# Expert fetches of 4 slots x 32 tokens in place of 1 slot x 128 tokens, with the weighting matmul in quarters

## The chip, the cores and the metric

One NeuronCore of one Trainium2 chip runs the whole program. The metric is device microseconds (us) of that core. The kernel before takes 4421.82 us, the median of three runs (4420.11 to 4427.95). All arithmetic is float32.

## The reference, cut to what matters

The program is one layer of a network over 9 tiles of 128 tokens (1 context tile, 8 latent tiles), D = 1024. Input projection, mLSTM and attention come first; the change touches only the last stage, `peer`, a retrieval of single-neuron experts:

```
q = (x @ w_q).reshape(N, 8, 256)                       # 8 heads
sa, sb = scores of the two halves of q against 128 keys each
va, ia = top_k(sa, 16);  vb, ib = top_k(sb, 16)        # "sides": 16 per token
cand = va[..., :, None] + vb[..., None, :]             # 256 candidates per head
top, pos = top_k(cand, 16);  eidx = ia*128 + ib at pos # 8 heads x 16 = 128 slots per token
gates = softmax(top)
a   = gelu(einsum('pd,phkd->phk', x, u_tab[eidx]))     # one dot product per token and slot
out = einsum('phk,phkd->pd', gates * a, v_tab[eidx])   # weighted sum of 128 rows per token
y   = x1 + gate2 * out
```

Each token thus reads 128 rows of u and 128 rows of v, 1024 floats each. They lie side by side in one table `uv` of 2048 floats a row, 8 KB.

## The kernel before, in words

The stage `peer` runs 9 tiles one after the other. A tile has 128 slots, done as 8 turns of 16 (`PAIR`). Slot i of a tile means: for each of the 128 tokens (one per partition) its i-th expert. One slot goes through these engines:

- GpSimd (POOL) copies 8 columns of indices (L1294) and issues one indirect DMA per slot (L1301). It gathers 128 rows of 8 KB, 1 MB, into one of 8 ring buffers (`ring`, `GROUP` = 8). Before it may issue, it waits for `s_pv`, which TensorE raises when the slot that used the buffer 8 slots earlier has been accumulated.
- VectorE (DVE) waits for the landing, multiplies the u half by the token's row in `h2` and sums it (L1528, one custom instruction and a read of the accumulator) to `dot`.
- Slots go on in batches of 2: ScalarE (ACT) applies gelu (L1407), VectorE multiplies by the gates (L1533), ScalarE makes one 128x128 diagonal matrix per slot, identity times the weight of each token (L1412).
- TensorE (PE) multiplies that diagonal by the v half of the ring buffer in two halves of 512 columns and adds into two PSUM accumulators `acc` (L1345). A float32 matmul is issued as two pairs of weight load and matmul, so that a slot is 4 matmul instructions. The second half raises `s_pv`.

Beside this, the engines prepare the retrieval of the next tile. TensorE does one query block of 8 matmuls (L1325) after each batch of 2 slots in the first 16 of the 64 batches of a tile, and 4 score blocks (L1336). VectorE takes one piece of top-k work (`next(work)`: L1452 to L1513) per batch, between the dot products of the batch and its product with the gates, from the fifth batch of turn 1 on. For tile 0 the retrieval runs ahead of the first fetch.

At a tile's end TensorE closes the accumulation (L1367), VectorE multiplies by `gate2` and adds the residual (L1554, L1556), SyncE (SP) stores y and loads the next x1 (L1266, L1268). The next tile's `h2` is loaded (L1264) into the one `h2` buffer when the last dot product of the tile is done; VectorE's next tile starts with a wait for it. Tiles 1 to 7 are one hardware loop; tiles 0 and 8 stand outside it.

The order of the work is written out by hand: each engine has its own instruction stream, and semaphores tie them. DMAs of SP and of POOL share the core's 16 DMA engines.

Of the kernel before, what the change touches and what calls it, by code (L numbers as in the profile page):

```python
# [14 lines left out]
P = 128  # L15
D = 1024
# [15 lines left out]
NEG = -1e30  # L32
C1 = P + 1


# [1134 lines left out]
def peer(nc, g, io):  # L1170
# [10 lines left out]
    with ExitStack() as ctx:  # L1181
# [15 lines left out]
        idf = sb("pe_idf", [P, NSIDE, TOPK])  # L1197
        cand = sb("pe_cand", [P, PH, TOPK * TOPK])
        crest = rest[:].rearrange("p (h s) k -> p h (s k)", s=2)
# [30 lines left out]
        s_sc = sem("pe_scores_ready")  # L1230
        s_top = sem("pe_sides_done")
        s_mid = sem("pe_dve_chain")
# [17 lines left out]
        with nc.Block() as block:  # L1250
            @block.sync
            def _(sp):
                flat = h2T[:].rearrange("p k n -> p (k n)")
                sp.dma_start(subT[:], io.subT).then_inc(s_small, 16)
                sp.dma_start(flat, g.h2T_dram[0]).then_inc(s_hT, 16)
                for k in range(KD):
                    sp.dma_start(w_q[:, k, :], io.w_q[k * P:(k + 1) * P, :]).then_inc(s_wq, 16)
                sp.dma_start(h2[:], g.h2_dram[0]).then_inc(s_h, 16)
# [12 lines left out]
                sp.dma_start(flat, g.h2T_dram[1]).then_inc(s_hT, 16)  # L1271
                with sp.Fori(0, TILES - 2) as t:
                    sp.wait_ge(s_q, t * NG + 2 * NG)
                    sp.dma_start(flat, g.h2T_dram[t + 2]).then_inc(s_hT, 16)
                    after(t)
                after(TILES - 2)
                sp.wait_ge(s_out, TILES)
                sp.dma_start(io.y[TILES - 1], x1[:]).then_inc(s_st, 16)
                sp.wait_ge(s_st, TILES * 16)

            @block.gpsimd
            def _(pool):
# [4 lines left out]
                def turn(t, r, first=False):  # L1287
                    n = t * TURNS + r
                    for half in range(2):
                        if not first:  # L1290

                            pool.wait_ge(s_dot, n * PAIR - PAIR + GROUP * (half + 1))
                            pool.sem_inc(g.s_tick, 1)
                        pool.tensor_copy(idg[half][:], g.eidx[:, t, bass.ds(r * PAIR + half * GROUP, GROUP)]).then_inc(s_idx, 1)  # L1294
                        pool.wait_ge(s_idx, n * 2 + (half + 1))
                        for j in range(GROUP):
                            i = half * GROUP + j
                            if not (first and half == 0):
# [17 lines left out]
            def _(pe):  # L1316
# [22 lines left out]
                def turn(t, r, retrieve=False):  # L1339
                    n = t * TURNS + r  # L1340
                    for i in range(PAIR):
                        pe.wait_ge(s_diag, n * PAIR + (i + 1))

                        for b in range(2):
                            mm = pe.matmul(acc[b][:], diag[:, i % GROUP, :], ring[i % GROUP][:, D + b * 512:D + (b + 1) * 512],  # L1345
                                           start=False, stop=False)
                        mm.then_inc(s_pv, 1)
                        m = r * NB + i // BATCH if retrieve else 0
                        if retrieve and i % BATCH == 1:

                            if m < NSIDE:
                                query(t + 1, m // 4, m % 4)
                            if m >= 7 and (m - 7) % 4 == 0 and (m - 7) // 4 < NG:
                                scores(t + 1, (m - 7) // 4)

# [13 lines left out]

                pe.wait_ge(s_const, 2)  # L1370
                pe.wait_ge(s_small, 16)
# [13 lines left out]
            def _(act):  # L1385
# [6 lines left out]
                def out(t, b, first=False):  # L1392
                    act.wait_ge(s_c, t * NG + (b + 1))
                    if not first:
                        act.wait_ge(s_top, t * NG + (b + 1 - NG))
                    act.activation(sc[:, 4 * b:4 * b + 4, :], cP[b % 2][:], ACT.Copy).then_inc(s_sc, 1)
# [5 lines left out]
                def turn(t, r, first=False, retrieve=False):  # L1402
                    n = t * TURNS + r
                    for q in range(NB):
# [4 lines left out]
                        for i in range(q * BATCH, (q + 1) * BATCH):  # L1409
                            if not (first and i < GROUP):  # L1410
                                act.wait_ge(s_pv, n * PAIR + (i - GROUP + 1))
                            act.activation(diag[:, i % GROUP, :], g.ident[:], ACT.Copy, scale=w[:, i:i + 1]).then_inc(s_diag, 1)  # L1412
                        m = r * NB + q if retrieve else 0
# [23 lines left out]
                out(0, NG - 1, True)  # L1437
                gate_exp(0)
                tile(0, True)
                with act.Fori(1, TILES - 1) as t:  # L1440
# [4 lines left out]
            def _(dve):  # L1445


                def top16(c, rows, src, left, v, ix, last_sem=None):

# [15 lines left out]
                    for r in rows[2:]:  # L1465
                        ins = dve.max_index(ix[:, r, 0:8], v[:, r, 0:8], src[:, r, :])
                        if last_sem is not None and r == end:
                            ins.then_inc(last_sem, 1)
                    for r in rows[:-1]:
# [4 lines left out]
                def retrieval(c, t):  # L1474
                    for b in range(NG):
                        dve.wait_ge(s_sc, t * NG + (b + 1))
                        dve.sem_inc(g.s_tick, 1)
                        yield from top16(c, range(4 * b, 4 * b + 4), sc, rest, val, idx, s_top)

                    v4 = val[:].rearrange("p (h s) k -> p h s k", s=2)  # L1480
                    c4 = cand[:].rearrange("p h (a b) -> p h a b", a=TOPK)
                    c.link(dve.tensor_tensor(c4, v4[:, :, 0, :].unsqueeze(3).to_broadcast([P, PH, TOPK, TOPK]),
# [14 lines left out]
                    i4 = idf[:].rearrange("p (h s) k -> p h s k", s=2)  # L1497
                    for side, hit in enumerate((cand[:], crest)):
                        h3 = hit.rearrange("p h (a b) -> p (h a) b", a=TOPK)
# [13 lines left out]
                    dve.tensor_tensor(g.gates[:, t, :].rearrange("p (h k) -> p h k", h=PH), gex[:],  # L1513
                                      gsum[:].unsqueeze(2).to_broadcast([P, PH, TOPK]), ALU.mult).then_inc(s_route, 1)
                    dve.wait_ge(s_route, t + 1)
# [20 lines left out]
                def tile(t, cnd, more=True):  # L1536
                    dve.wait_ge(s_h, t * 16 + 16)
                    dve.sem_inc(g.s_tick, 1)
# [16 lines left out]
                    dve.wait_ge(s_gated, t * 2 + 2)  # L1555
                    dve.tensor_tensor(x1[:], x1[:], gated[:], ALU.add).then_inc(s_out, 1)  # L1556

                dve.wait_ge(s_const, 2)
                c = Count(dve, s_mid, LINKS, 0, g.s_tick)
# [172 lines left out]
```

## Time and profile before

| | |
|---|---|
| median of three runs | 4421.82 us |
| span of the profiled execution, first to last instruction | 4419.0 us |
| the profiled execution's own time | not listed apart from its span |
| stage `peer`, from the first fetch to the end | 1389.7 to 4419 us |
| indirect fetches | 1152, 1208.03 MB |
| PE busy, whole span | 3525.3 us (80%) |
| DVE / ACT / POOL busy | 2394.0 / 887.8 / 1616.3 us |

The profile page is one execution. Its 40 slices give, for each engine, the busy share in tenths. "PEclk" is TensorE's granted clock as a share of 2.4 GHz, "DMA" the mean busy share of the 16 DMA engines, and "GB/s" what they moved. "Idle before" is the time an engine stood still ahead of an instruction, with what released it. A busy share of the whole span mixes stages; the tables by window show one stage at a time.

### The profile page before, as it was taken

How to read it: one execution, taken by the hardware profiler on the slowest of the kernel's cores; microseconds unless marked ns; L12 is line 12 of the kernel's file. 1: busy time of each engine (PE TensorE's matmuls, PEld its weight loads, DVE VectorE, ACT ScalarE, POOL GpSimd, SP SyncE). 2: the span in 40 equal slices, each digit the busy share in tenths (PEclk: the TensorE clock that was granted, in tenths of full speed). 3: DMA queues.
4: the chain of work that ended last, by engine and by line, in shares of the span. 5: the costliest groups of instructions: out<-in, count | busy, mean ns of one | idle time of the engine just before them, and what ended most of it. 6: DMA issues, size and time to landing. Idle time of an engine off the chain costs nothing.

```text
span 4419.0 us, 43120 instructions
## 1 busy us (share of the span) xinstructions
PE 3525.3 (80%) x11157; PEld 1783.5 (40%) x11157; DVE 2394.0 (54%) x5673; ACT 887.8 (20%) x2523; POOL 1616.3 (37%) x1434
## 2 busy tenths in 40 slices
PE   8899778888864878877977977977977977977777
PEld 1444366555543423423523523522522522522222
DVE  1232354333316675674684685685584585585554
ACT  1111123322311221121121221121121121222111
POOL 0000011111102454454454454454445455445554
PEclk9899877777777999999999999999999999999999
DMA  9101123111134999999999999999999999999998
GB/s 368 56 34 45 55 92 119 38 47 38 47 125 172 410 418 417 404 419 387 403 416 390 400 417 391 398 420 397 391 418 417 371 418 420 372 420 417 415 421 360
DMA packets 219388, 1343.70 MB, mean 304 GB/s; under 512 B 22938, under 2 KB 33818, under 8 KB 69786
## 3 DMA queue, kind: packets, MB, share of 16 engines
q0 software_dynamic: 165888, 1208.03, 66.9%
q1 hardware_dynamic: 45628, 108.76, 6.8%
q10 hardware_dynamic: 7776, 25.96, 1.5%
q14 instruction: 75, 0.61, 0.0%
q8 instruction: 21, 0.34, 0.0%
HBM read 1311.33 MB, written 31.33 MB: 304 GB/s over the span
## 4 chain that ended last, share of the span: by engine, by line
DMA 30%; PE 22%; issue 9%; DVE 5%; POOL 3%; ACT 1%; POOLq 0%; DVEq 0%; SPq 0%; ACTq 0%
DMA pe_ring<-arg_uv,pe_fetch_idx 29%; PE pe_acc L1345 16%; PE pe_qP L1325 6%; POOL pe_ring L1301 3%; DVE pe_ring L1528 1%; ACT pe_diag L1412 1%; PE pe_cP L1336 1%; DVE pe_ab L1507 1%; DVE pe_rest L1456 0%; DMA pe_w_q<-arg_w_q 0%; DVE pe_w L1533 0%; DVE pe_cand L1501 0%; DVE pe_rest L1504 0%; ACT pe_gelu L1407 0%; PE pe_acc L1367 0%
## 5 line engine op out<-in xcount | busy, mean ns | idle before, releaser
L1345 PE MATMUL pe_acc<-pe_ring,pe_diag 128*128 128x512 f32 x4608 | 2145.1, 610 | 649.6 <-ACT pe_diag L1412 649.6
L1301 POOL DMA_INDIRECT pe_ring<-arg_uv,pe_fetch_idx x1152 | 1434.4, 1245 | 1509.0 <-PE pe_acc L1345 1358.3
L1528 DVE CUSTOM_DVE_ANT_0 pe_ring<-pe_ring,pe_h 128x1024 f32<-128x1024 f32 x1152 | 1407.0, 1226 | 845.9 <-DMA pe_ring<-arg_uv,pe_fetch_idx 813.0
L1345 PEld LDWEIGHTS pe_acc<-pe_ring,pe_diag 128*128 128x128 f32 x4608 | 845.0, 193 | 1851.4 <-ACT pe_diag L1412 996.8
L1412 ACT ACTIVATE pe_diag<-ident,pe_w 128x128 f32<-128x128 f32 x1152 | 399.5, 394 | 622.1 <-DVE pe_w L1533 597.9
L1407 ACT ACTIVATE pe_gelu<-pe_dot 128x2 f32<-128x2 f32 x576 | 117.1, 203 | 1822.3 <-DVE pe_dot L1528 1822.2
L348 PE MATMUL in_z<-w_in,in_hT 128*128 128x512 f32 (+1 forms) x864 | 356.7, 575 | 22.3 <-ACT in_hT L378 22.3
L1325 PEld LDWEIGHTS pe_qP<-pe_h2T,pe_w_q 128*128 128x128 f32 x2304 | 279.6, 193 | 90.0 <-issue 90.0
L1325 PE MATMUL pe_qP<-pe_h2T,pe_w_q 128*128 128x128 f32 x2304 | 280.4, 276 | 28.1 <-DMA pe_w_q<-arg_w_q 28.1
L348 PEld LDWEIGHTS in_z<-w_in,in_hT 128*128 128x128 f32 x864 | 168.3, 196 | 205.6 <-issue 197.9
L1533 DVE TENSOR_TENSOR pe_w<-pe_gelu,gates 128x2 f32<-128x2 f32 x576 | 92.4, 160 | 187.3 <-ACT pe_gelu L1407 116.6
L945 POOL TENSOR_TENSOR at_h<-at_h,at_hrms 128x512 f32<-128x512 f32 x9 | 9.4, 1040 | 450.5 <-DVE at_hrms L1120 450.5
L1014 PE MATMUL at_uP<-at_w_out,at_mixT 128*128 128x512 f32 x288 | 143.9, 658 | 0.9 <-DVE at_mixT L1137 0.9
L1104 DVE CUSTOM_DVE_ANT_0 at_s<-at_sP,at_mask,at_sink 128x512 f32<-128x512 f32 x72 | 54.0, 749 | 153.0 <-PE at_sP L967 149.1
L316 POOL COPY in_turned<-in_heads 128x320 f32<-128x320 f32 x9 | 4.0, 450 | 361.4 <-DVE in_heads L449 361.4
L1294 POOL COPY pe_fetch_idx<-eidx 128x8 uint32 (+1 forms) x144 | 60.9, 423 | 107.7 <-DVE gates L1513 106.8
L1049 ACT ACTIVATE at_pT<-at_tP 128x512 f32<-128x512 f32 x72 | 43.0, 597 | 268.3 <-PE at_tP L975 268.3
L474 DVE COPY att_kT<-in_akTp 128x256 f32 (+1 forms) x9 | 3.8, 425 | 170.4 <-PE in_akTp L365 170.4
L163 PE MATMUL ada_acc<-ada_w,ada_silu 128*2 128x512 f32 x192 | 84.5, 601 | 14.3 <-DMA ada_w<-arg_w_ada 14.3
L1528 DVE DVE_READ_ACCUMULATOR2_ANT pe_dot<- 128x1 f32 x1152 | 95.4, 83 | 0.0
L975 PE MATMUL at_tP<-ident,at_p 128*128 128x128 f32 x288 | 67.2, 376 | 32.2 <-ACT at_p L1044 32.2
L1014 PEld LDWEIGHTS at_uP<-at_w_out,at_mixT 128*128 128x128 f32 x288 | 60.1, 215 | 72.0 <-issue 70.9
(255 smaller groups left out, 2440.5 us busy)
## 6 DMA issues: line engine op xcount, KB each, us to landing
ada_w<-arg_w_ada SPq DMA_DIRECT2D x12, 2048.0 KB, 10.2
pe_ring<-arg_uv,pe_fetch_idx POOLq DMA_INDIRECT x1152, 11.4
w_in<-arg_w_in SPq DMA_DIRECT2D x8, 1416.0 KB, 20.8
ml_qkT<-qkT_scratch SPq DMA_DIRECT2D x18, 512.0 KB, 3.5
pe_w_q<-arg_w_q SPq DMA_DIRECT2D x8, 1024.0 KB, 12.7
ada_x<-arg_x ACTq DMA_DIRECT2D x9, 512.0 KB, 6.4
in_xn<-arg_x SPq DMA_DIRECT2D x9, 512.0 KB, 3.7
kv_scratch<-in_kv ACTq DMA_DIRECT2D x9, 512.0 KB, 2.6
```

The source lines that it names most:

```text
L163: mm = pe.matmul(acc[j][0:COND, :], silu[:, k, :], wbuf[j][:, k, :], start=(k == 0), stop=(k == KD - 1))
L348: mm = pe.matmul(zp[b % 3][:, 0:n], hT[:, k, :], g.w_in[:, k, c0:c0 + n], start=(k == 0), stop=(k == KD - 1))
L975: mm = pe.transpose(tP[h % 2][:, j * P:(j + 1) * P], p[h % 2][:, j * P:(j + 1) * P], g.ident[:])
L1014: mm = pe.matmul(uP[2 - 2 * half][:], mixT[:, k, :], w_out[:, k, half * 512:(half + 1) * 512], start=(k == 0), stop=(k == KD - 1))
L1294: pool.tensor_copy(idg[half][:], g.eidx[:, t, bass.ds(r * PAIR + half * GROUP, GROUP)]).then_inc(s_idx, 1)
L1301: pool.indirect_dma_start(out=ring[j][:], out_offset=None, in_=io.uv, in_offset=bass.IndirectOffsetOnAxis(ap=idg[half][:, j:j + 1], axis=0 ...
L1325: mm = pe.matmul(qP[b % 2][:, j, :], w_q[:, k, i * P:(i + 1) * P], h2T[:, k, :], start=(k == 0), stop=(k == KD - 1))
L1345: mm = pe.matmul(acc[b][:], diag[:, i % GROUP, :], ring[i % GROUP][:, D + b * 512:D + (b + 1) * 512], start=False, stop=False)
L1407: act.activation(gelu[:, sl], dot[:, sl], ACT.Gelu_apprx_tanh).then_inc(s_gelu, 1)
L1412: act.activation(diag[:, i % GROUP, :], g.ident[:], ACT.Copy, scale=w[:, i:i + 1]).then_inc(s_diag, 1)
L1528: dve.tensor_tensor_reduce(out=ring[j][:, 0:D], in0=ring[j][:, 0:D], in1=h2[:], scale=1.0, scalar=0.0, op0=ALU.mult, op1=ALU.add, accum_ou ...
L1533: dve.tensor_tensor(w[:, sl], gelu[:, sl], g.gates[:, t, bass.ds(r * PAIR + q * BATCH, BATCH)], ALU.mult).then_inc(s_w, 1)
```

## The change: what it does

There are `NC` = 4 token groups of `TOKS` = 32 tokens. A fetch now serves one token group (cg = i % 4) and four slots at once: partition s*32 + t of ring buffer i holds token cg*32 + t, slot s*32 + i//4. Four fetches in a row cover all 128 tokens for four slots. The number and size of fetches is the same.

For this the indices and the gates are written permuted, in 16 small instructions each (32 partitions, 32 elements) in place of one each; `h2` becomes four buffers, each with one token group's rows repeated four times, loaded by 16 DMAs of 128 KB each in place of one of 512 KB; the diagonal is 128x32, made from `pick` (four stacked 32x32 identities); and each weighting matmul writes 32 partitions of the accumulator. TensorE waits for the diagonals of four fetches and raises `s_pv` once for the four, so that ring buffers come free four at a time. `cand` now lies in the storage of the scores, `gated` in that of `rest`; ScalarE's copy of new scores waits for `s_route`.

```diff
+NC = 4
+TOKS = P // NC
+SPAN = SLOTS // NC
-        cand = sb("pe_cand", [P, PH, TOPK * TOPK])
+        cand = sc[:].rearrange("p (h s) k -> p h (s k)", s=2)
-        h2 = sb("pe_h2", [P, D])
+        h2 = [sb(f"pe_h2_{i}", [P, D]) for i in range(NC)]
-        gated = sb("pe_gated_sum", [P, D])
+        gated = rest[:].rearrange("p h k -> p (h k)")[:, 0:D]
-        diag = sb("pe_diag", [P, GROUP, P])
+        diag = sb("pe_diag", [P, GROUP, TOKS])
+        pick = sb("pe_pick", [P, TOKS])
...
+                def tokens(t):
+                    for cg in range(NC):
+                        for s in range(NC):
+                            sp.dma_start(h2[cg][s * TOKS:(s + 1) * TOKS, :], g.h2_dram[t, cg * TOKS:(cg + 1) * TOKS, :]
+                                         ).then_inc(s_h, 16)
...
                     sp.wait_ge(s_dot, t * SLOTS + SLOTS)
-                    sp.dma_start(h2[:], g.h2_dram[t + 1]).then_inc(s_h, 16)
+                    tokens(t + 1)
...
                             if not (first and half == 0):
-                                pool.wait_ge(s_pv, n * PAIR + (i - GROUP + 1))
+                                pool.wait_ge(s_pv, n * (PAIR // NC) + ((i - GROUP) // NC + 1))
...
-                    for i in range(PAIR):
-                        pe.wait_ge(s_diag, n * PAIR + (i + 1))
+                    for i in range(0, PAIR, NC):
+                        pe.wait_ge(s_diag, n * PAIR + (i + NC))
                         for b in range(2):
-                            mm = pe.matmul(acc[b][:], diag[:, i % GROUP, :], ring[i % GROUP][:, D + b * 512:D + (b + 1) * 512],
-                                           start=False, stop=False)
+                            for cg in range(NC):
+                                j = (i + cg) % GROUP
+                                mm = pe.matmul(acc[b][cg * TOKS:(cg + 1) * TOKS, :], diag[:, j, :],
+                                               ring[j][:, D + b * 512:D + (b + 1) * 512], start=False, stop=False)
                         mm.then_inc(s_pv, 1)
...
-                            act.activation(diag[:, i % GROUP, :], g.ident[:], ACT.Copy, scale=w[:, i:i + 1]).then_inc(s_diag, 1)
+                            act.activation(diag[:, i % GROUP, :], pick[:], ACT.Copy, scale=w[:, i:i + 1]).then_inc(s_diag, 1)
...
-                    c.link(dve.scalar_tensor_tensor(g.eidx[:, t, :], ab[:, 0, :], float(P), ab[:, 1, :], ALU.mult, ALU.add))
+                    for cg in range(NC):
+                        for s in range(NC):
+                            to = g.eidx[s * TOKS:(s + 1) * TOKS, t, :].rearrange("p (k c) -> p k c", c=NC)[:, :, cg]
+                            of = ab[cg * TOKS:(cg + 1) * TOKS, :, s * SPAN:(s + 1) * SPAN]
+                            ins = dve.scalar_tensor_tensor(to, of[:, 0, :], float(P), of[:, 1, :], ALU.mult, ALU.add)
+                    c.link(ins)
...
+                    HS = PH // NC
+                    for cg in range(NC):
+                        for s in range(NC):
+                            ...
+                            ins = dve.tensor_tensor(to, gex[part, s * HS:(s + 1) * HS, :],
+                                                    gsum[part, s * HS:(s + 1) * HS].unsqueeze(2).to_broadcast([TOKS, HS, TOPK]),
+                                                    ALU.mult)
...
-                            dve.tensor_tensor_reduce(out=ring[j][:, 0:D], in0=ring[j][:, 0:D], in1=h2[:],
+                            dve.tensor_tensor_reduce(out=ring[j][:, 0:D], in0=ring[j][:, 0:D], in1=h2[i % NC][:],
...
+                dve.tensor_reduce(pick[:], g.ident[:].rearrange("p (s t) -> p t s", s=NC), AX.X, ALU.add).then_inc(s_const, 1)
```

## Rows read from the trace of the kernel before

**Rows 1.** Busy time by stretch: PE, PEld, DVE, ACT, POOL, granted clock, DMA share, GB/s.
```profile
1740.00:1820.00 80.00, 80.00 (x383) 51.91 (x382) 45.61 (x118) 15.17 (x48) 36.74 (x34) 1.00 1.00 396
2080.00:2160.00 80.00, 80.00 (x383) 51.90 (x382) 44.08 (x116) 14.97 (x47) 36.46 (x34) 1.00 0.99 385
...
1960.00:2040.00 80.00, 61.19 (x131) 24.08 (x130) 42.04 (x80) 16.91 (x50) 45.95 (x38) 0.98 1.01 420
2060.00:2080.00 20.00, 12.37 (x35) 6.21 (x36) 11.54 (x22) 3.59 (x12) 2.82 (x3) 0.83 0.76 290
```
**Rows 2.** Chain of waits, one trip round the ring: start, length, what.
```profile
1641.36 2.00 PE pe_acc L1345 x4
...
1644.15 0.96 POOL pe_ring L1301
...
1646.38 13.57 DMA pe_ring<-arg_uv,pe_fetch_idx
...
1662.20 2.00 PE pe_acc L1345 x4
```
**Rows 3.** Timeline of the steady stretch: start, length, instruction, idle before it.
```profile
2045.83 1.23 DVE L1528 CUSTOM_DVE_ANT_0 pe_ring<-pe_ring,pe_h 128x1024 f32<-128x1024 f32 x1 [1.26 <-DMA pe_ring<-arg_uv,pe_fetch_idx]
...
2047.72 0.69 ACT L1412 ACTIVATE pe_diag<-ident,pe_w 128x128 f32<-128x128 f32 x2 [0.41 <-DVE pe_w L1533]
2048.17 3.70 PE L1345 MATMUL pe_acc<-pe_ring,pe_diag 128*128 128x512 f32 x8 [1.27 <-ACT pe_diag L1412]
...
2050.82 1.23 DVE L1528 CUSTOM_DVE_ANT_0 pe_ring<-pe_ring,pe_h 128x1024 f32<-128x1024 f32 x1 [1.27 <-DMA pe_ring<-arg_uv,pe_fetch_idx]
```
**Rows 4.** The fetch line L1301: durations, and time from issue to landing.
```profile
L1301 POOL DMA_INDIRECT pe_ring<-arg_uv,pe_fetch_idx x1152: 932/940/2600, 1389.7 to 4393.0; - x192
DMA to landing us min/median/max: 5.4/11.4/18.3
```
**Rows 5.** Timeline: TensorE after a short and after a long idle time.
```profile
2019.80 0.34 PEld L1345 LDWEIGHTS pe_acc<-pe_ring,pe_diag 128*128 128x128 f32 x1 [0.39 <-issue]
2020.66 0.34 PEld L1345 LDWEIGHTS pe_acc<-pe_ring,pe_diag 128*128 128x128 f32 x1 [0.52 <-issue]
...
2069.58 5.93 PE L1345 MATMUL pe_acc<-pe_ring,pe_diag 128*128 128x512 f32 x8 [7.63 <-ACT pe_diag L1412]
...
2408.28 5.54 PE L1345 MATMUL pe_acc<-pe_ring,pe_diag 128*128 128x512 f32 x8 [7.59 <-ACT pe_diag L1412]
...
2747.31 6.69 PE L1345 MATMUL pe_acc<-pe_ring,pe_diag 128*128 128x512 f32 x8 [7.57 <-ACT pe_diag L1412]
```
**Rows 6.** Chain of waits where VectorE does a piece of top-k.
```profile
1538.75 1.23 DVE pe_ring L1528
1540.51 0.78 DVE pe_idx L1470 x3
1542.48 2.00 PE pe_acc L1345 x4
...
1599.15 1.23 DVE pe_ring L1528
1600.38 2.22 DVE pe_cand L1504
1603.46 2.00 PE pe_acc L1345 x4
```
**Rows 7.** Timeline: TensorE in the query stretch.
```profile
2080.56 1.95 PE L1325 MATMUL pe_qP<-pe_h2T,pe_w_q 128*128 128x128 f32 x16
2082.35 3.60 PE L1345 MATMUL pe_acc<-pe_ring,pe_diag 128*128 128x512 f32 x8
```
**Rows 8.** Timeline of one tile's end.
```profile
2052.24 0.33 SPq L1264 DMA_DIRECT2D pe_h<-h_scratch  x1
...
2066.09 1.23 DVE L1528 CUSTOM_DVE_ANT_0 pe_ring<-pe_ring,pe_h 128x1024 f32<-128x1024 f32 x1 [4.92 <-issue]
...
2074.17 0.96 POOL L1301 DMA_INDIRECT pe_ring<-arg_uv,pe_fetch_idx  x1 [15.36 <-PE pe_acc L1345]
```
**Rows 9.** SP's DMAs: the h2 load's landing, and eight loads issued in a row.
```profile
DMA to landing us min/median/max: 7.7/7.8/8.0
...
L1257 SPq DMA_DIRECT2D pe_w_q<-arg_w_q x8: 424/440/521, 1282.0 to 1285.5; - x8
```
**Rows 10.** VectorE's small instructions, grouped by line.
```profile
L1512 DVE RECIPROCAL pe_gsum<-pe_gsum 128x8 f32<-128x8 f32 x8 | 1.6, 204 | 1.2
L1509 DVE SCALAR_TENSOR_TENSOR eidx<-pe_ab 128x128 f32 x7 | 2.0, 288 | 0.0
L1456 DVE MATCH_VALUE_LOAD pe_rest<-pe_val,pe_scores 128x8 f32 x96 | 8.0, 83 | 0.0
```

More of the change, by code:

```diff
@@ L1230, in peer @@
         s_sc = sem("pe_scores_ready")
-        s_top = sem("pe_sides_done")
         s_mid = sem("pe_dve_chain")
@@ L1257, in _ @@
                     sp.dma_start(w_q[:, k, :], io.w_q[k * P:(k + 1) * P, :]).then_inc(s_wq, 16)
-                sp.dma_start(h2[:], g.h2_dram[0]).then_inc(s_h, 16)
+                def tokens(t):
[3 more added lines that the diff above has]
+                                         ).then_inc(s_h, 16)
+                tokens(0)
                 sp.dma_start(x1[:], g.x1_dram[0]).then_inc(s_x, 16)
@@ L1340, in turn @@
                     n = t * TURNS + r
-                    for i in range(PAIR):
-                        pe.wait_ge(s_diag, n * PAIR + (i + 1))
+                    for i in range(0, PAIR, NC):
+                        pe.wait_ge(s_diag, n * PAIR + (i + NC))
                         for b in range(2):
-                            mm = pe.matmul(acc[b][:], diag[:, i % GROUP, :], ring[i % GROUP][:, D + b * 512:D + (b + 1) * 512],
-                                           start=False, stop=False)
+                            for cg in range(NC):
+                                j = (i + cg) % GROUP
+                                mm = pe.matmul(acc[b][cg * TOKS:(cg + 1) * TOKS, :], diag[:, j, :],
+                                               ring[j][:, D + b * 512:D + (b + 1) * 512], start=False, stop=False)
                         mm.then_inc(s_pv, 1)
[L1348 to L1354, printed above, removed]
+                        if retrieve:
+                            for m in range(r * NB + i // BATCH, r * NB + (i + NC) // BATCH):
+                                if m < NSIDE:
+                                    query(t + 1, m // 4, m % 4)
+                                if m >= 7 and (m - 7) % 4 == 0 and (m - 7) // 4 < NG:
+                                    scores(t + 1, (m - 7) // 4)
                 def tile(t, first=False, more=True):
@@ L1368, in tile @@
                     mm.then_inc(s_acc, 1)
-                pe.wait_ge(s_const, 2)
+                pe.wait_ge(s_const, 3)
                 pe.wait_ge(s_small, 16)
@@ L1394, in out @@
                     if not first:
-                        act.wait_ge(s_top, t * NG + (b + 1 - NG))
+                        act.wait_ge(s_route, t)
                     act.activation(sc[:, 4 * b:4 * b + 4, :], cP[b % 2][:], ACT.Copy).then_inc(s_sc, 1)
@@ L1410, in turn @@
                             if not (first and i < GROUP):
-                                act.wait_ge(s_pv, n * PAIR + (i - GROUP + 1))
-                            act.activation(diag[:, i % GROUP, :], g.ident[:], ACT.Copy, scale=w[:, i:i + 1]).then_inc(s_diag, 1)
+                                act.wait_ge(s_pv, n * (PAIR // NC) + ((i - GROUP) // NC + 1))
+                            act.activation(diag[:, i % GROUP, :], pick[:], ACT.Copy, scale=w[:, i:i + 1]).then_inc(s_diag, 1)
                         m = r * NB + q if retrieve else 0
@@ L1438, in _ @@
                 gate_exp(0)
+                act.wait_ge(s_const, 3)
                 tile(0, True)
@@ L1445, in _, with top16 @@
             def _(dve):
-                def top16(c, rows, src, left, v, ix, last_sem=None):
+                def top16(c, rows, src, left, v, ix):
                     end = rows[-1]
@@ L1465, in top16 @@
                     for r in rows[2:]:
-                        ins = dve.max_index(ix[:, r, 0:8], v[:, r, 0:8], src[:, r, :])
-                        if last_sem is not None and r == end:
-                            ins.then_inc(last_sem, 1)
+                        dve.max_index(ix[:, r, 0:8], v[:, r, 0:8], src[:, r, :])
                     for r in rows[:-1]:
@@ L1477, in retrieval @@
                         dve.sem_inc(g.s_tick, 1)
-                        yield from top16(c, range(4 * b, 4 * b + 4), sc, rest, val, idx, s_top)
+                        yield from top16(c, range(4 * b, 4 * b + 4), sc, rest, val, idx)
                     v4 = val[:].rearrange("p (h s) k -> p h s k", s=2)
-                    c4 = cand[:].rearrange("p h (a b) -> p h a b", a=TOPK)
+                    c4 = cand.rearrange("p h (a b) -> p h a b", a=TOPK)
                     c.link(dve.tensor_tensor(c4, v4[:, :, 0, :].unsqueeze(3).to_broadcast([P, PH, TOPK, TOPK]),
@@ L1497, in retrieval @@
                     i4 = idf[:].rearrange("p (h s) k -> p h s k", s=2)
-                    for side, hit in enumerate((cand[:], crest)):
+                    for side, hit in enumerate((cand, crest)):
                         h3 = hit.rearrange("p h (a b) -> p (h a) b", a=TOPK)
@@ L1512, in retrieval @@
                     c.link(dve.reciprocal(gsum[:], gsum[:]))
-                    dve.tensor_tensor(g.gates[:, t, :].rearrange("p (h k) -> p h k", h=PH), gex[:],
-                                      gsum[:].unsqueeze(2).to_broadcast([P, PH, TOPK]), ALU.mult).then_inc(s_route, 1)
+                    HS = PH // NC
+                    for cg in range(NC):
+                        for s in range(NC):
+                            to = g.gates[s * TOKS:(s + 1) * TOKS, t, :].rearrange("p (h k c) -> p h k c", h=HS, c=NC)[:, :, :, cg]
+                            part = slice(cg * TOKS, (cg + 1) * TOKS)
+                            ins = dve.tensor_tensor(to, gex[part, s * HS:(s + 1) * HS, :],
+                                                    gsum[part, s * HS:(s + 1) * HS].unsqueeze(2).to_broadcast([TOKS, HS, TOPK]),
+                                                    ALU.mult)
+                    ins.then_inc(s_route, 1)
                     dve.wait_ge(s_route, t + 1)
@@ L1536, in tile @@
                 def tile(t, cnd, more=True):
-                    dve.wait_ge(s_h, t * 16 + 16)
+                    dve.wait_ge(s_h, t * (16 * NC * NC) + 16 * NC * NC)
                     dve.sem_inc(g.s_tick, 1)
@@ L1555, in tile @@
                     dve.wait_ge(s_gated, t * 2 + 2)
-                    dve.tensor_tensor(x1[:], x1[:], gated[:], ALU.add).then_inc(s_out, 1)
-                dve.wait_ge(s_const, 2)
+                    dve.tensor_tensor(x1[:], x1[:], gated, ALU.add).then_inc(s_out, 1)
+                dve.tensor_reduce(pick[:], g.ident[:].rearrange("p (s t) -> p t s", s=NC), AX.X, ALU.add).then_inc(s_const, 1)
+                dve.wait_ge(s_const, 3)
                 c = Count(dve, s_mid, LINKS, 0, g.s_tick)
```

## The prediction

> **What bounds the kernel now.** I read the table of stretches first. Where no retrieval matmuls run (64 slots and more of each tile), the 16 DMA engines are busy all the time at 420 GB/s, while TensorE is busy 61.2 of 80 us and VectorE 42.0 [rows 1]. A fetch moves 1,048,576 bytes, so a slot costs 2.49 us, which is half the 4.99 us between dot products of the same place in two batches [rows 3]. So the bound is the fetch traffic: 1152 x 2.49 = 2872 us of the 3029 us of the stage. Relieving TensorE can win only where the DMA engines are not full. That is the query stretch, the first 16 batches of tiles 0 to 7: TensorE is busy 80 of 80 us and the rate falls to 396 and 385 GB/s [rows 1], since two slots and a query block take 3.60 + 1.95 less their overlap [rows 7], 5.2 us in place of 4.99. Against 420 GB/s the 80 us lose about 6 us, 48 us for eight tiles. The other place is the tile's end, 290 GB/s over 20 us [rows 1].
>
> The chain of waits goes round the ring: fetch, dot product, gelu, gates, diagonal, TensorE, next fetch into the same buffer [rows 2]. A trip takes 8 x 2.49 = 19.95 us. Of it the fetch takes some 12 us because it queues behind others; the least from issue to landing is 5.4 us [rows 4]. This queueing of about 6.5 us is all the reserve there is, and the change spends it.
>
> **The ring with four buffers freed at a time.** The loop for a group of four is:
> - issue to the landing of the fourth: 5.4 + 3 x 2.49 = 12.9 us [rows 4, 3];
> - landing to TensorE's start: the dot product begins at 2045.83, the matmuls at 2048.17 [rows 3], 2.3 us, and the second diagonal 0.35 us later, somewhat less with 32 columns: 2.6;
> - TensorE for the four: G;
> - its end to the next issue: 2.79 us from the matmul's start to the fetch's issue [rows 2], less 4 x 0.43: 1.1.
>
> That is 16.6 + G us per 8 slots (two groups share the ring), against 19.95. The DMA engines stay full only while G is at most 3.4 us; above that every microsecond is lost 144 times (1152/8). Before, half the slots waited for one partner and TensorE took them one by one.
>
> **G.** A float32 matmul of 512 columns is two instructions, spaced 0.43 us at 2.4 GHz (8 in 3.70 us [rows 3]) and 0.86 us at 1.2 GHz (weight loads at 2019.80 and 2020.66 [rows 5]). Four fetches are 16 instructions. The columns that stream are as many as before, so the narrower diagonal alone saves nothing. Only running quarters beside one another would, and no row of the trace shows that. The ends: no overlap, 16 x 0.43 = 6.9 us; full overlap of four, 4 x 0.43 = 1.7 us. Between: the two instructions of one matmul go to the same quarter, so if instructions start in order, the second waits for the first, and only it overlaps the next quarter's first. Then 8 matmuls take 9 steps, 3.9 us. I take this.
>
> The Trainium skill (TensorEngine Tiling (Array Packing), Key Properties) says that tiles run independently, in parallel, which would be the full overlap. The Trainium skill (TensorE: Matmul & The Clock Gate, Part 3: Packing small matmuls) gives 2.38 times for three column tiles, and says that matmuls start and end strictly in order. No run here shows either. By the first rule the sum would be rival A's, by the second, with two instructions per matmul, the middle case.
>
> **The clock.** TensorE now stands still 1.3 us between bursts and keeps 2.4 GHz (0.98 to 1.00 [rows 1]); after 7.6 us of standing still, eight instructions took 5.93, 5.54 and 6.69 us in place of 3.70 [rows 5], 2.3 us more on the mean. After the change a burst comes every 10 us or more and the gap is 6 us or so. So outside the query stretch I add 2.3: G = 6.2. In the query stretch (32 of 144 trips: a trip is 4 batches, 16 batches in each of eight tiles) queries fill the gaps and G stays 3.9.
>
> **The sum**, against the span of 4419.0 us:
> - 112 trips at 16.6 + 6.2 = 22.8 us, 2.85 more: +319. 32 trips at 20.5: +17.
> - VectorE's top-k pieces lie between the last dot product and the gates. From dot product to TensorE it is 3.7 us with a small piece and 4.3 with a large one, against 2.3 [rows 6, 3]: 1.5 us on the mean. Queueing hid it; with no reserve left it shows. 33 pieces per tile are 8.25 trips, x 8 tiles x 1.5: +99.
> - TensorE's excess in the query stretch goes: 16 x (3.9/2 + 1.95) fits in the fetch time: -48.
> - Tile ends, 8. h2 becomes 2 MB by 16 DMAs. SP's issues alone take 16 x 0.44 = 7 us [rows 9]; 0.5 MB landed in 7.8 us beside the fetches [rows 9], so 2 MB take between 10 us and the 25 us in which all that is in flight (eight fetches and 2 MB at 420 GB/s) must have landed. I take 20 us after the last dot product. Before, VectorE began 14 us after it (2052.1 to 2066.1 [rows 8], of which 4.92 us are no wait for data, the loop's jump back, now hidden): +6, and +11 at the two ends without the jump, 7.2 on the mean. The first refill before came 8.1 us after VectorE's start (2066.09 to 2074.17 [rows 8]); now it takes four dot products and diagonals, 6.6, + G 6.2 + 1.1, 13.9: +5.8. Together 13.0 x 8: +104.
> - 32 small VectorE instructions for indices and gates in place of two of 0.29 us: 83 ns to 204 ns each [rows 10], 2.7 to 6.5 us; taken at 4.1, less 0.6, x 9 tiles: +31. The nearest row by shape is the 204 ns one, which waits for the instruction before; these do not.
> - The last group at the end: +3.
> - At nothing: pick, the extra wait of ScalarE for `s_route` (raised a tile earlier), the storage shared by cand and gated (their old contents are used up by then), h2's first load (it lies beside tile 0's retrieval, from 1285.5 [rows 9] to the first fetch at 1389.7 [rows 4]; SP has only x1 behind it).
>
> +525: 4944 us of span. The page gives no time of the execution beside its span; the median of the runs is 2.8 us above it: **4947**. Its own range is 4750 to 5100 (issue to landing up to 1 us longer, +144; the clock kept at 2.4 GHz, 112 x 2.3 = 258 at most).
>
> **Rivals.**
> - A, full overlap at 1.2 GHz, bursts all slow: G = 3.4. Trips 20.04: +10. Pieces +99, queries -48, ends 8 x (7.2 + 3.0) = +82, small +31: 4419 + 174 + 2.8 = **4596**, up to 4740 if landing is 1 us longer. For it: the quarters are separate outputs with separate inputs. Against it: the two instructions per quarter.
> - B, no overlap: G = 9.2 (6.9 + 2.3), trips 25.8, 5.85 more x 112: +655; 32 x 3.55: +114; +99, -48, ends 8 x 16.0 = +128, +31, +5: **5406**. For it: no row shows any overlap of matmuls, and 0.43 us each is what every float32 instruction of 512 columns takes.
> - C, faster: full overlap and the clock stays at 2.4 GHz: G = 1.7, a trip of 18.3 leaves 1.6 us of reserve, enough for the 1.5 of the pieces. It decides at G of about 1.9. The query stretch gives -48; if h2 lands before VectorE is back, the ends cost 8 x 1.3 = +10, and the small instructions only ahead of tile 0, +3: **4387**. For it: 290 GB/s at the tile's end leave room for 1.5 MB. Against it: the clock after gaps of 7.6 us [rows 5].
> - D, all of it within what the reserve hides: the gain and the tile ends cancel, 4415 to 4430. A narrow case between A and C.
>
> **Chances.** Forecast 0.42, A 0.28, B 0.14, C 0.11, D 0.05. What a measurement here can tell from no change is 0.2%, 9 us. Faster is C: 0.11; same is D, 0.04 of it within 9 us; slower the rest, 0.85. The 8-in-10 range leaves out C below and the upper half of B: 4440 to 5300.
>
> **What would show it.** DMA GB/s in the stretch without retrieval falls from 420 to about 365 (forecast), stays near 418 (A), or falls to 325 (B). The median from issue to landing falls from 11.4 us towards 7 to 9. The burst of 16 matmuls spans 6 us and its granted clock is well under 1. The query stretch reaches 410 GB/s. h2 lands about 20 us after the last dot product. The forecast is wrong if 16 weighting matmuls span under 4 us, or if TensorE keeps 2.4 GHz between bursts; then A or C holds, and the loss is in the top-k batches and the tile ends.

## The result and the profile after

The changed kernel takes 4912.34 us (median of four runs, 4906.38 to 4913.94) against 4422.9 us before: ratio 1.1105, 95% interval 1.1091 to 1.1119. The forecast was 4947 us. The profiled execution took 4906.38 us, its span 4904.5 us, so 485.5 us more than before's span.

The sum came out close, but several of its terms were wrong, in opposite directions. First the table of stretches of the kernel after, columns as in [rows 1]: a quarter of a tile with queries, a tile's end, and (last row) a plain stretch of the last tile.
```profile
2189.00:2272.00 83.00, 53.96 (x369) 35.04 (x370) 47.16 (x114) 14.20 (x53) 30.98 (x31) 0.81 0.85 334
...
2160.00:2200.00 40.00, 13.16 (x45) 4.05 (x46) 12.42 (x23) 2.90 (x13) 4.99 (x6) 0.59 0.77 251
4630.00:4800.00 170.00, 53.71 (x240) 8.94 (x240) 81.33 (x156) 22.81 (x93) 68.97 (x70) 0.57 0.97 379
```
Where the fetches ran at 420 GB/s they now run at 379, and TensorE is busy 54 of 170 us at 0.57 of its clock. The lightened engine was not the bound; the transfers lost their full queue.

The timeline of one trip round the ring in that plain stretch, as [rows 3]:
```profile
4651.25 1.80 POOL L1311 DMA_INDIRECT pe_ring<-arg_uv,pe_fetch_idx  x1 [4.76 <-PE pe_acc L1357]
...
4653.51 1.23 DVE L1550 CUSTOM_DVE_ANT_0 pe_ring<-pe_ring,pe_h 128x1024 f32<-128x1024 f32 x1 [0.73 <-DMA pe_ring<-arg_uv,pe_fetch_idx]
...
4656.01 1.23 DVE L1550 CUSTOM_DVE_ANT_0 pe_ring<-pe_ring,pe_h 128x1024 f32<-128x1024 f32 x1 [1.26 <-DMA pe_ring<-arg_uv,pe_fetch_idx]
...
4659.35 1.23 DVE L1550 CUSTOM_DVE_ANT_0 pe_ring<-pe_ring,pe_h 128x1024 f32<-128x1024 f32 x1 [1.57 <-DMA pe_ring<-arg_uv,pe_fetch_idx]
...
4666.87 1.22 DVE L1550 CUSTOM_DVE_ANT_0 pe_ring<-pe_ring,pe_h 128x1024 f32<-128x1024 f32 x1 [1.30 <-DMA pe_ring<-arg_uv,pe_fetch_idx]
...
4669.26 3.64 PE L1357 MATMUL pe_acc<-pe_ring,pe_diag 128*32 128x512 f32 x16 [7.35 <-ACT pe_diag L1423]
...
4673.74 1.76 POOL L1311 DMA_INDIRECT pe_ring<-arg_uv,pe_fetch_idx  x1 [6.12 <-PE pe_acc L1357]
```
Read it as the forecast's loop: issue at 4651.25, first landing 8.1 us later (forecast 5.4), three more at 2.5 us, the fourth's dot product at 4666.87, TensorE 2.4 us after it, next issue 4.5 us after TensorE's start. Together 22.5 us; the forecast had 22.8 and before took 19.95. The burst of 16 matmuls takes 3.64 us, not 6.2. The dot products at 4653.51 and 4656.01 belong to the other group of four: its last two fetches were still in flight when this group's first was issued, and the first landed 3.3 us after the last of them.

The weight loads of one burst show how the sixteen run:
```profile
4680.84 0.20 PEld L1357 LDWEIGHTS pe_acc<-pe_ring,pe_diag 128*32 128x32 f32 x8 [9.67 <-ACT pe_diag L1423]
...
4681.69 0.20 PEld L1357 LDWEIGHTS pe_acc<-pe_ring,pe_diag 128*32 128x32 f32 x4 [0.66 <-issue]
```
Eight at once (this and the next step of four quarters), then four every 0.86 us (the last four at 4682.55), the spacing of 1.2 GHz [rows 5]: four quarters in step, four steps of 0.86 us. The ends of matmuls in these profiles are modelled, but GpSimd's next issue bears them out: it comes 4.5 us after the burst's start (4669.26 to 4673.74), which sixteen steps would not allow.

The tile's end, as [rows 8], from the timeline; the last dot product of the tile ends at 2159.8:
```profile
2159.97 7.42 SPq L1265 DMA_DIRECT2D pe_h<-h_scratch  x16
...
2188.95 1.23 DVE L1550 CUSTOM_DVE_ANT_0 pe_ring<-pe_ring,pe_h 128x1024 f32<-128x1024 f32 x1 [18.79 <-DMA pe_h<-h_scratch]
...
2199.82 0.96 POOL L1311 DMA_INDIRECT pe_ring<-arg_uv,pe_fetch_idx  x1 [28.65 <-PE pe_acc L1357]
...
2205.56 1.22 DVE L1550 CUSTOM_DVE_ANT_0 pe_ring<-pe_ring,pe_h 128x1024 f32<-128x1024 f32 x1 [5.17 <-DMA pe_ring<-arg_uv,pe_fetch_idx]
```
The sixteen h2 loads are issued in 7.4 us, but the last copy lands 29 us after the last dot product, and the first refill comes 40 us after it (22 before). This is the shortest of the eight ends: in the others VectorE starts 32 to 34 us after the last dot product. The refill of 2199.82, issued into an empty queue, has its dot product 5.7 us later. In groups by line, VectorE waits for h2 181.1 us in all, and the small instructions take 209 ns (indices, shown) and 207 ns (gates):
```profile
L1550 DVE CUSTOM_DVE_ANT_0 pe_ring<-pe_ring,pe_h 128x1024 f32<-128x1024 f32 x1151 | 1403.7, 1225 | 1267.1 <-DMA pe_ring<-arg_uv,pe_fetch_idx 1083.1 <-DMA pe_h<-h_scratch 181.1 <-issue 1.6
...
L1523 DVE SCALAR_TENSOR_TENSOR eidx<-pe_ab 32x32 f32 (+1 forms) x128 | 26.8, 209 | 1.6
```

From the starts of the 1152 dot products each tile can be cut into quarters of 32 slots (us; q1 to q4 are means of tiles 0 to 7, q4 counts to the last start; "end" is from the last start of a tile to the first of the next; "plain" is the mean of q2 and q3 in tile 8, which prepares no retrieval):

| kernel | q1 (queries) | q2 | q3 (top-k) | q4 | end | plain |
|---|---|---|---|---|---|---|
| before | 81.1 | 83.3 | 80.4 | 78.3 | 14.0 | 79.8 |
| after | 83.7 | 93.5 | 97.4 | 85.1 | 33.5 | 87.7 |
| e1: before, fours | 89.9 | 94.5 | 96.5 | 86.1 | 14.1 | 89.2 |
| e2: after, pairs | 77.1 | 82.6 | 83.3 | 79.0 | 32.7 | 79.8 |
| e5: after, 0.5 MB of h2 | 83.9 | 94.3 | 98.1 | 85.7 | 15.8 | 88.7 |
| e7: after, fill matmuls | 84.0 | 93.8 | 95.2 | 83.3 | 33.9 | 86.0 |
| e10: pairs and 0.5 MB | 77.7 | 82.8 | 83.4 | 79.0 | 14.7 | 79.8 |
| e11: before, queries spread | 77.3 | 83.2 | 82.4 | 77.1 | 14.0 | 79.8 |

The first dot product comes between 1392 and 1407 us in all kernels run, e3 to e9 too (one execution of each). That spread lies ahead of the stage and is not the change's; it blurs differences of 10 us between kernels of few runs.

### The profile page after: what moved, and what is told of

Its sections match the earlier page's. It is cut to its first block, busy times and chain, and to the rows that moved or that the text cites. A ratio compares the mean times of both kernels' runs of the same rounds, so it can differ in the third digit from the quotient of the medians.

```text
span 4904.5 us, 41983 instructions
## 1 busy us (share of the span) xinstructions
PE 2436.9 (50%) x11157; PEld 1125.9 (23%) x11157; DVE 2449.2 (50%) x5944; ACT 795.6 (16%) x2523; POOL 1473.7 (30%) x1434
## 4 chain that ended last, share of the span: by engine, by line
DMA 34%; issue 13%; PE 11%; DVE 8%; POOL 5%; ACT 1%; SPq 1%; POOLq 0%; DVEq 0%; ACTq 0%
DMA pe_ring<-arg_uv,pe_fetch_idx 30%; PE pe_acc L1357 10%; POOL pe_ring L1311 5%; DMA pe_h<-h_scratch 4%; DVE pe_ring L1550 3%; SPq L1265 1%; ACT pe_diag L1423 1%; PE pe_qP L1335 1%; DVE pe_w L1555 1%; DVE pe_rest L1468 1%; DMA pe_w_q<-arg_w_q 0%; DVE pe_pos L1480 0%; ACT pe_gelu L1418 0%; DVE pe_rest L1511 0%; DVE pe_top L1464 0%
## 5 line engine op out<-in xcount | busy, mean ns | idle before, releaser
L1357 PE MATMUL pe_acc<-pe_ring,pe_diag 128*32 128x512 f32 x4608 | 990.9, 1008 | 2222.2 <-ACT pe_diag L1423 2222.2
L1311 POOL DMA_INDIRECT pe_ring<-arg_uv,pe_fetch_idx x1152 | 1303.9, 1132 | 2133.6 <-PE pe_acc L1357 1857.9
L1357 PEld LDWEIGHTS pe_acc<-pe_ring,pe_diag 128*32 128x32 f32 x4608 | 166.9, 154 | 2943.1 <-ACT pe_diag L1423 2586.4
L1423 ACT ACTIVATE pe_diag<-pe_pick,pe_w 128x32 f32<-128x32 f32 x1152 | 307.0, 313 | 652.5 <-DVE pe_w L1555 652.5
L1335 PE MATMUL pe_qP<-pe_h2T,pe_w_q 128*128 128x128 f32 x2304 | 301.2, 293 | 29.5 <-DMA pe_w_q<-arg_w_q 29.5
L986 PE MATMUL at_aP<-att_v,at_pT 128*128 (+1 forms) x432 | 87.5, 360 | 0.0
L1304 POOL COPY pe_fetch_idx<-eidx 128x8 uint32 (+1 forms) x144 | 48.8, 339 | 115.1 <-DVE gates L1533 114.5
```

What stands on the lines that cost most here:

```text
L986: mm = pe.matmul(aP[:, h * ADH:(h + 1) * ADH], pT[h % 2][:, j * P:(j + 1) * P], rhs, start=(j == 0), stop=(j == 3))
L1335: mm = pe.matmul(qP[b % 2][:, j, :], w_q[:, k, i * P:(i + 1) * P], h2T[:, k, :], start=(k == 0), stop=(k == KD - 1))
L1357: mm = pe.matmul(acc[b][cg * TOKS:(cg + 1) * TOKS, :], diag[:, j, :], ring[j][:, D + b * 512:D + (b + 1) * 512], start=False, stop=False)
L1423: act.activation(diag[:, i % GROUP, :], pick[:], ACT.Copy, scale=w[:, i:i + 1]).then_inc(s_diag, 1)
```

## Experiments

**e1. The kernel before, buffers freed in fours.**
```diff
-pool.wait_ge(s_pv, n * PAIR + (i - GROUP + 1))
+pool.wait_ge(s_pv, n * PAIR + ((i - GROUP) // 4 * 4 + 4))
```


> The kernel before, with one thing changed: a fetch may be issued only when the whole group of four buffers it belongs to has been accumulated. Layout, diagonals and matmuls stay as before, 128x128. The last two slots of a group take TensorE 2 x 1.72 = 3.4 us after their diagonals, about what the changed kernel's burst takes (3.64 us). Theory 1 (the loss comes from freeing the buffers in fours, and the first fetch of four takes 8 us to land, as in the changed kernel, not 5.4): a trip round the ring is 22 us or so, the stretch without retrieval falls from 420 to 370-385 GB/s, and the time is 4700 to 4820 us. Theory 2 (the loss comes from the quarter layout: fetches of 4 slots x 32 tokens or the narrow matmuls slow the transfers): this kernel stays within 1% of before, 4420 to 4460 us, at 418-420 GB/s.

Measured 4811.37 us (ratio 1.0868, 1.084 to 1.0895). No quarter, no narrow matmul, no new h2 load, and the plain stretch falls to 376 GB/s, beside 421 in a plain stretch of the kernel before:
```profile
4540.00:4710.00 170.00, 121.56 (x243) 48.27 (x244) 80.86 (x154) 27.82 (x93) 69.20 (x70) 0.93 0.97 376
```
Its q2 to q4 and its plain quarter are within 2 us of the changed kernel's. So the release in fours, alone, costs 384 us, beside 489 for the whole change, each against before in its own series of runs. The parts do not simply add: this kernel's heavier TensorE makes q1 worse than the changed kernel's, and it has none of the longer tile ends. Its trace has the landing of two fetches in eight only, always the same two places: their median is 8.8 us, as at these places in the changed kernel. Theory 1 holds.

**e2. The changed kernel with TensorE and the release in pairs.** ScalarE's wait for `s_pv` and the range of the query batches go to twos as well.
```diff
-for i in range(0, PAIR, NC):
-    pe.wait_ge(s_diag, n * PAIR + (i + NC))
+for i in range(0, PAIR, 2):
+    pe.wait_ge(s_diag, n * PAIR + (i + 2))
...
-        for cg in range(NC):
-            j = (i + cg) % GROUP
+        for k in range(2):
+            j, cg = (i + k) % GROUP, (i + k) % NC
...
-pool.wait_ge(s_pv, n * (PAIR // NC) + ((i - GROUP) // NC + 1))
+pool.wait_ge(s_pv, n * (PAIR // 2) + ((i - GROUP) // 2 + 1))
```


> The changed kernel, with TensorE taking two fetches (two quarters) at a time as soon as their two diagonals are there, and raising the semaphore once per two; everything else (layout, sixteen h2 loads, small instructions) stays. Theory 1: the ring has its reserve back, the stretch without retrieval returns to 420 GB/s; what remains over before are the tile ends (about +15 us each, 8 of them, +120) and a part of the small instructions (+0 to +20), less the query stretch (-48): 4480 to 4530 us. Theory 2: the rate stays near 365 GB/s and the time above 4750 us.

Measured 4564.77 us (ratio 1.0305, 1.0284 to 1.0327), 35 us above the range given. The plain stretch is back at the transfers' full rate, and TensorE's clock there is 0.77:
```profile
4325.00:4475.00 150.00, 83.65 (x244) 13.94 (x242) 79.40 (x151) 22.09 (x90) 76.57 (x69) 0.77 1.01 420
```
So the slow clock costs nothing once the reserve is there, and fetches of 4 slots x 32 tokens are as fast as any. q1 is 4 us shorter than before: there the lighter TensorE does win. What remains is above all the tile's end, 32.7 us (150 us over eight tiles), and 2.9 us in q3.

**e3. All quarters into one.** `acc[b][cg * TOKS:(cg + 1) * TOKS, :]` becomes `acc[b][0:TOKS, :]`.

> The changed kernel with all four matmuls of a group written to the first quarter of the accumulator's partitions, so three quarters of the output are left out; instructions and bytes are the same. If the overlap of matmuls comes from their lying in different quarters: sixteen instructions in a row, 13.7 us at 1.2 GHz or about 9.2 us with the clock coming back, 5.6 us or more added to each trip outside the query stretch, 5500 to 5800 us. If any narrow matmuls overlap: 3.64 us per burst and 4900 to 4920 us.

Measured 5504.85 us (one run). Two bursts in the timeline:
```profile
5207.39 8.36 PE L1357 MATMUL pe_acc<-pe_ring,pe_diag 128*32 128x512 f32 x16 [9.95 <-ACT pe_diag L1423]
5217.40 7.05 PE L1357 MATMUL pe_acc<-pe_ring,pe_diag 128*32 128x512 f32 x16 [1.65 <-ACT pe_diag L1423]
```
In place of 3.64 us. The overlap comes from the quarters being different; this is rival B's kernel, and B's 5406 us was 2% short of it. The edit also makes all sixteen add into the same 32 partitions of the accumulator; a wait of each for the sum of the one before would look the same, and no run separates the two.

**e4. The loops over quarters and halves swapped.** `for cg` outside, `for b` inside: four instructions in a row go to one quarter.

> The changed kernel with the two loops of the weighting matmuls swapped: both halves of one quarter follow each other, four instructions in one quarter before the next quarter's. If instructions start strictly in order, only the last of a quarter overlaps the next quarter's first: 13 steps, 11 us at 1.2 GHz and 7 to 8 with the clock coming back, 5300 to 5500 us. If each quarter runs its own instructions independently of the order: 4 steps as now, 3.64 us per burst, 4900 to 4920 us.

Measured 4938.96 us (one run, of which 8 us lie ahead of the first fetch). The bursts take 3.67 us:
```profile
4644.32 3.67 PE L1357 MATMUL pe_acc<-pe_ring,pe_diag 128*32 128x512 f32 x16 [6.72 <-ACT pe_diag L1423]
```
The time is 19 us above the range given, and 13 steps would be 11 us at this clock. From a burst's start to GpSimd's next issue it is 4.5 us, as in the changed kernel. Each quarter runs its own instructions, whatever the order across quarters. The forecast's middle case, two at a time, does not exist here.

**e5. 0.5 MB of h2 in place of 2 MB** (from tile 1 on the loop over copies runs once).

> The changed kernel, but from tile 1 on h2 is loaded by four DMAs of 128 KB (the first of the four copies of each token group), 0.5 MB in place of 2 MB; the other three copies keep tile 0's rows, so part of the dot products is of wrong tokens. Theory 1 (the sixteen loads set the start of each tile): the first dot product comes 15 to 18 us after the last one of the tile before, not 30 to 35; the ring is then less full at the start, so of the 16 us about 11 are won per end: 4805 to 4830 us. Theory 2 (the ring's own refill hides them): within 20 us of 4905.

Measured 4783.95 us (ratio 1.0807, 1.0787 to 1.0828), 128 us less; the end falls from 33.5 to 15.8 us and nothing is given back in q1 (83.9). The time is below the range of theory 1: its 11 us per end were too low, 128 us are 16 per end.

**e6. Indices and gates by one instruction each.**
```diff
-for cg in range(NC):
-    for s in range(NC):
-        to = g.eidx[s * TOKS:(s + 1) * TOKS, t, :] ...
+c.link(dve.scalar_tensor_tensor(g.eidx[:, t, :], ab[:, 0, :], float(P), ab[:, 1, :], ALU.mult, ALU.add))
...
```
The gates, not shown, are written by one instruction in the same way.

> The changed kernel with indices and gates written by one instruction each, as before the change, so without the permutation: fetches get the rows of other slots and tokens, of the same number and size. If the 32 small instructions show in full, 6.7 less 0.6 us for each of nine tiles: -50 us, about 4860. If they lie in time in which VectorE would wait anyway: -5 to -25 us, 4885 to 4905.

Measured 4895.19 us (ratio 1.1059, 1.1042 to 1.1077), 17 us less, of which the first dot product's place (1392 us, 1398 in the changed kernel) is 6: of some 55 us of added VectorE work a third at most shows; q3 falls by 2.3 us per tile.

**e7. Fill matmuls to hold the clock.**
```diff
+if not retrieve:
+    for k in range(6):
+        pe.matmul(fill[0:TOKS, :], zero[:, 0:TOKS], zero[:], start=True, stop=True)
```


> The changed kernel with six matmuls of 512 columns on zeros into a spare PSUM bank after each group's burst, outside the query stretch, to keep TensorE's clock at 2.4 GHz; results are untouched. Theory 1 (each microsecond of the burst is paid once per trip): the burst falls from 3.64 to 1.9 us, the trip by 1.7 us, 112 trips: -190 us, 4710 to 4740, at about 400 GB/s. Theory 2 (the transfers are what limits at 370 GB/s, the fetch lands later by what the burst saves): 4890 to 4915 us.

Measured 4879.38 us (ratio 1.1023, 1.1002 to 1.1044), only 33 us less; the plain stretch moves 389 GB/s at a clock of 0.88. Two bursts in its timeline:
```profile
2096.88 3.64 PE L1358 MATMUL pe_acc<-pe_ring,pe_diag 128*32 128x512 f32 x16 [5.26 <-ACT pe_diag L1427]
...
2106.84 1.92 PE L1358 MATMUL pe_acc<-pe_ring,pe_diag 128*32 128x512 f32 x16 [0.89 <-ACT pe_diag L1427]
```
In the plain stretch the fill keeps the clock for every second burst only. A burst there takes 2.7 us on the mean in place of 3.6, and the plain quarter falls by 1.7 us, 0.4 per trip: half of what the burst saves. (The fill stands in the last five of a tile's eight turns and in all of tile 8, 96 trips, not 112.) Inconclusive between the two theories: neither number was met. What the clock would be worth if every burst had it was not measured.

**e8 and e9. Why does the first of four land after 8 us?** e8 computes the dot products over 512 of 1024 columns; e9 fetches adjacent rows (`near`, an iota) in place of the chosen ones.

> The changed kernel with VectorE's dot products over the first 512 of the 1024 columns; the other half of each is left out. It shortens the way from landing to TensorE by 0.55 us and halves the time in which VectorE is busy while GpSimd issues (its issues last 0.94 us alone, 1.3 to 1.9 beside a dot product). Theory 1 (the first fetch of four lands after 8 us because the transfers start again from an emptied queue): landing stays at 7.5 to 8 us, the trip falls by 0.6 to 0.8 us: 4790 to 4840 us. Theory 2 (the issues are held up by VectorE): landing falls to 6.5 us or less, the trip by 2 us: 4600 to 4680 us.

> The changed kernel with the fetched rows replaced by fixed, adjacent ones: partition p of ring buffer j gets row 128 j + p, so all results of the experts are of other rows; number and size of the transfers are the same. Theory 1 (the loss lies in the drained queue whatever rows are read): within 1% of 4912 us. Theory 2 (rows spread over the table make the 16 engines finish unevenly when few fetches are queued): the first fetch lands in about 6.5 us and the trip falls by 1.5 us or more, 4680 to 4780 us.

e8: 4813.97 us (ratio 1.0878, 1.085 to 1.0906), 98 us less, 388 GB/s in the plain stretch. From the issue of the first of four to its dot product, the median in the plain stretch is 7.9 us (8.1 in the changed kernel, 7.7 in e1, 12.3 before): VectorE does not hold up the issues, and what is won is 0.7 us per trip on the mean (98 us over 144 trips), 0.4 in the plain quarter (87.7 to 86.0). e9: 4943.02 us (ratio 1.1169, 1.1141 to 1.1198), 377 GB/s, 7.7 us: the rows play no part. Theory 2 fails in both.

But theory 1 has its mechanism wrong too: the queue is not empty when the first of four is issued. The trace of the changed kernel settles it. Of its 286 fetches that are the first of four, the median from issue to landing goes by how many others are in flight at the issue: 5.6 us with none (16 fetches), 6.1 with one (30), 7.5 with two (185), 8.8 with three (49) and 11.2 with four (6). In the plain stretch the last fetch of the other group lands 4.3 us after the issue, on the mean, and the first of four 3.4 us after that; the steps to the second, third and fourth are 2.7, 2.5 and 2.5. Four landings thus take 11.1 us, where 2.49 us each would make 10.0: this is 378 GB/s in place of 420.

**e10. Pairs and 0.5 MB of h2 together.**

> Release in pairs and 0.5 MB of h2 together: TensorE takes two fetches at a time, and from tile 1 on h2 is loaded by four DMAs (three of four copies stay those of tile 0, so part of the dot products is of wrong tokens). If the two causes, buffers freed in fours and the h2 load at the tile's end, are all there is beside the small instructions: 4564 less 8 x 17 = 4420 to 4440 us, level with before. If a third cause is left: above 4470.

Measured 4430.49 us (ratio 1.0017, 1.0006 to 1.0028). The two causes account for the loss but for 7 us, which is no more than the spread ahead of the stage. This level is a balance: over eight tiles q1 is 27 us shorter than before (81.1 to 77.7), while q3, q4 and the ends are 35 us longer, of which the small instructions may be some 18 (e6: 2.3 us in q3).

**e11. A version faster than both: the kernel before with the queries spread over 24 batches.**
```diff
-if m < NSIDE:
-    query(t + 1, m // 4, m % 4)
-if m >= 7 and (m - 7) % 4 == 0 and (m - 7) // 4 < NG:
-    scores(t + 1, (m - 7) // 4)
+k = m // 3 * 2 + m % 3
+if m % 3 < 2 and k < NSIDE:
+    query(t + 1, k // 4, k % 4)
+if m >= 8 and (m - 8) % 6 == 0 and (m - 8) // 6 < NG:
+    scores(t + 1, (m - 8) // 6)
```


> The kernel before, with the 16 query blocks of the next tile spread over 24 batches (two batches in three) in place of 16, the score blocks, ScalarE's copies and VectorE's top-k work moved later to match. It takes from the kernel before the only loss that the change's lighter TensorE could win back, without touching the ring. If TensorE's excess in the query stretch is what costs there: the quarters of a tile with queries and top-k (81 and 83.3 us per 32 slots) approach 79.8, 3 to 5 us per tile, 4380 to 4400 us. If that excess is made up later by the ring in any case: 4415 to 4425 us.

Measured 4398.78 us (ratio 0.9939, 0.9924 to 0.9953): faster than before by 0.6%, near the upper end of the first range. q1 falls from 81.1 to 77.3 and q4 by 1.2, q3 rises by 2.0: 3.0 us per tile.

## Why the prediction came out right, and where it did not

- **The bound and the direction: right.** The transfers at 420 GB/s set the time before; e2 and e10 show the same rate with the quarter layout in place.
- **The ring's reserve: right, and shown.** Freeing the buffers in fours alone costs 384 us (e1); in pairs the plain stretch loses nothing (e2).
- **G, the burst: wrong.** The forecast's "if instructions start in order, the second waits for the first" failed. Bursts are 3.64 us, the full overlap of rival A at 1.2 GHz; e3 shows that the quarters make it, e4 that the order does not matter. Of the two rules of the Trainium skill that stood behind the choice, the one on tiles that run independently (TensorEngine Tiling (Array Packing), Key Properties) agrees with e4. The other rule of the Trainium skill, strict order of starts and ends (TensorE: Matmul & The Clock Gate, Part 3: Packing small matmuls), does not: by it e4's bursts would take 11 us, and they take 3.67. The 2.38 times for three tiles that the same section gives, 0.79 per tile, is short of what these bursts show: sixteen steps of 0.86 us, 13.8 us, in 3.64 us, 3.8 times for four quarters.
- **Issue to landing: mis-sized the other way.** The 5.4 us came from a lone fetch into an empty queue, and such a fetch still takes 5.6 us. The sum took each group of four by itself; what failed is that it put the other group's fetches, which share the DMA engines, at nothing. Two of them are ahead of the first of four as a rule (e8 and e9). So it took 8.1 us, 2.7 us more per trip than the sum had, against 2.6 us less for G. So the trip came to 22.5 us in the timeline and 21.9 on the mean (87.7/4) beside 22.8 forecast: two errors that cancel. A's G with the right landing time makes 22.7 us per trip. The forecast named a burst under 4 us as the sign that A or C holds; the burst is under 4 us, and yet the plain stretch moves 379 GB/s and not A's 418, for A had the same landing time.
- **The clock: right that it falls** (0.57 in place of 1.00), but it is priced through G, which was wrong; e7 won 33 us with every second burst at the full clock, and e2 runs at 0.77 at no cost in the plain stretch.
- **The query stretch: wrong sign.** Forecast -48 + 17, measured +21 (83.7 less 81.1, eight tiles). The relief is there in e2 (77.1), and the release in fours takes it back. It was over-sized as well: e2 gains 37 us in q1 and q2 and has lost 29 of them again by the end of q4, and e11, which takes the relief alone, gains 24 us in all. The stretch moved 334 GB/s over its quarter (400 from 2205 to 2265 us, once the refill had come), where 410 were forecast.
- **Top-k pieces and small instructions:** forecast +99 and +31. Above the plain quarter q2 and q3 have 5.8 + 9.7 us per tile, 124 us for eight; before had 3.5 + 0.6 us, 33 us for eight, so that 91 us are the change's, against 130. The small instructions are at the upper end of their bound (209 ns, 6.7 us per tile), but mostly hidden (e6: 17 us).
- **Tile ends: mis-sized.** h2 was taken at 20 us after the last dot product, with 25 as the latest; VectorE started 29 to 34 us after it. The end grew by 19.5 us, 156 us in all, where 7.2 us each, 58 us, were forecast; the other 46 of the 104 us were for a later first refill, which came 10.9 us after VectorE's start in place of 8.1, not 13.9. The bound of 25 us assumed that all in flight moves at 420 GB/s; the 40 us of the end moved 251.
- **Sum by quarters, 8 tiles:** +21 (q1), +82, +136, +54, ends +156, tile 8 +32, start +2: 483 of 485.5 us. That the total is near 525 is luck: the trips outside the query stretch cost 2.0 us each over 19.95 (87.7/4) where 2.85 were forecast, 98 us less, and the starts after the tile ends cost 98 us more than forecast.

Left open: why the first of four lands 3.4 us after the last fetch of the other group, and not 2.5, although it was issued 4.3 us ahead of that landing. VectorE's load and the rows read are excluded (e8, e9); how the 16 engines take up a short queue was not measured.

## What to carry to other kernels

When the transfers are the bound, the queueing time of a fetch is the reserve of the ring, and a change that frees buffers in larger groups spends it, however cheap the group's work becomes; compute the trip with what the other groups still have in flight ahead of the fetch, not with a lone fetch. Four matmuls into four quarters of the partitions do run nearly four times as fast, but take the group only as large as the ring can wait for: pairs kept the 420 GB/s. Two errors can cancel in a sum, so check its terms against the trace even when the total fits.

## What the hardware showed that was not expected

- float32 matmuls of 128x32 into different quarters overlap fully, with distinct moving data and two instructions per matmul: 16 in 3.64 us at 1.2 GHz and in 1.92 us at 2.4 GHz; into one quarter the same 16 take 7.05 us at 2.4 GHz and up to 10.0 where the granted clock was lower. The order across quarters is free (3.67 us).
- 2 MB in sixteen DMAs beside the fetches in flight have landed 29 to 34 us after the last dot product; 0.5 MB in four bring the end back to 15.8 us.
- A fetch of 128 rows of 8 KB lands 5.6 us after its issue with no other in flight, 7.5 with two, 8.8 with three and 11.4 with a full ring [rows 4].
- A VectorE instruction on 32 partitions x 32 elements takes 207 to 209 ns, where 128 x 128, sixteen times as many elements, takes 288 ns [rows 10].
